# Products of zeros in TensorE's first waits, earlier column sums and a new place for one modulation tile per quarter, in a two-block transformer kernel

## The reference, cut to what matters

```python
c_act = jax.nn.silu(c)                                   # c: (1, 1024)
mod = jnp.einsum('bd,de->be', c_act, w_ada[l]) + b_ada[l]    # w_ada: (1024, 6 * 1024)
shift_m, scale_m, gate_m, shift_f, scale_f, gate_f = [m[:, None, :] for m in jnp.split(mod, N_MOD, axis=-1)]
h = (_rms(x) * (1.0 + scale_m) + shift_m).astype(dt)     # x: (1, 256, 1024)
proj = jnp.einsum('bsd,de->bse', h, w_in[l])             # w_in: (1024, 4104)
...
```

## Time and profile before

| | |
|---|---|
| median of 3 runs | 1022.15 us (1015.5 to 1022.82) |
| profiled execution, its own time | 1015.01 us |
| its span in the profile | 1013.2 us |
| TensorE busy (matmul) | 951.8 us, 94% |
| VectorE, ScalarE, GpSimd busy | 656.6, 485.2, 53.9 us |
| mean granted TensorE clock | 0.992 |
| read from HBM | 185.13 MB, 184 GB/s over the span |

### The profile page before, as it was taken

One profiled execution on the slowest core, in us unless ns is written; L12 is line 12 of the kernel. 1 busy time (PEld: TensorE's weight loads), 2 busy tenths in 40 slices (PEclk: granted clock), 3 DMA queues, 4 the chain that ended last, 5 costly groups with the idle time before them and its releaser, 6 DMA issues.

```text
span 1013.2 us, 14870 instructions
## 1 busy us (share of the span) xinstructions
PE 951.8 (94%) x5572; PEld 816.1 (81%) x5572; DVE 656.6 (65%) x828; ACT 485.2 (48%) x734; POOL 53.9 (5%) x59
## 2 busy tenths in 40 slices
PE   3889979799999999999899999998999989999996
PEld 3767867599999987977689999996776879999995
DVE  5778897886545575666884555558544876554555
ACT  5456646455444444444354544443653735444540
POOL 3030101100000001000020000001000010000000
PEclk9999989999999999999999999999999999999998
DMA  9998776776665576411476556544442447566531
GB/s 285 300 244 287 206 205 231 254 239 220 198 198 185 167 268 153 134 67 59 125 214 230 167 186 201 193 167 147 144 149 100 125 167 249 171 198 206 172 125 42
DMA packets 109991, 186.94 MB, mean 184 GB/s; under 512 B 8696, under 2 KB 67088, under 8 KB 109920
## 3 DMA queue, kind: packets, MB, share of 16 engines
q1 hardware_dynamic: 104800, 177.33, 54.2%
q0 software_dynamic: 2592, 8.53, 3.0%
q10 hardware_dynamic: 2544, 0.35, 0.2%
HBM read 185.13 MB, written 1.05 MB: 184 GB/s over the span
## 4 chain that ended last, share of the span: by engine, by line
PE 78%; DVE 9%; ACT 4%; issue 3%; DMA 2%; POOL 2%; SPq 0%; POOLq 0%; ACTq 0%; DVEq 0%
PE PJ L1766 14%; PE PJ L1767 13%; PE PJ L1768 13%; PE AT L1908 9%; PE AT L1907 9%; PE AT L1906 9%; DVE wlo L1107 2%; POOL rstd L467 2%; PE AT L1992 1%; DMA raw<-in_w_out_dram 1%; PE AT L2035 1%; PE AT L1757 1%; DMA raw<-in_w_in_dram 1%; DVE bn L1192 1%; DVE acc L1130 1%
## 5 line engine op out<-in xcount | busy, mean ns | idle before, releaser
L1107 DVE TENSOR_TENSOR wlo<-raw,whi 128x1024 fp32r<-128x1024 f32 x144 | 172.7, 1220 | 53.4 <-ACT whi L581 52.9
L1906 PE MATMUL AT<-hT_hi,whi 128*128 128x256 f32 x720 | 203.8, 283 | 0.0
L1908 PE MATMUL AT<-hT_hi,wlo 128*128 128x256 f32 x720 | 203.8, 283 | 0.0
L1907 PE MATMUL AT<-hT_lo,whi 128*128 128x256 f32 x720 | 203.7, 283 | 0.0
L1235 DVE TENSOR_TENSOR wlo<-raw,whi 128x1024 fp32r<-128x1024 f32 x144 | 169.8, 1221 | 33.1 <-ACT whi L639 32.6
L1766 PE MATMUL PJ<-whi,uhi 128*128 128x512 f32 x432 | 170.3, 394 | 1.7 <-DVE wlo L1107 0.9
L581 ACT ACTIVATE whi<-raw 128x1024 fp32r<-128x1024 f32 x144 | 146.7, 1054 | 49.4 <-DMA raw<-in_w_in_dram 29.3
L1767 PE MATMUL PJ<-wlo,uhi 128*128 128x512 f32 x432 | 168.7, 390 | 0.0
L1768 PE MATMUL PJ<-whi,ulo 128*128 128x512 f32 x432 | 168.2, 389 | 0.0
L639 ACT ACTIVATE whi<-raw 128x1024 fp32r<-128x1024 f32 x144 | 144.4, 1049 | 48.2 <-PE PJ L1768 44.3
L1766 PE MATMUL PJ<-whi,hT_hi 128*128 128x512 f32 (+1 forms) x320 | 132.3, 413 | 11.4 <-DVE hT_lo L1283 7.3
(11 more groups left out here) (310 smaller groups left out, 1054.8 us busy)
## 6 DMA issues: line engine op xcount, KB each, us to landing
raw<-in_mlp_w_dram SPq DMA_DIRECT2D x128, 512.0 KB, 4.9
raw<-in_w_in_dram SPq DMA_DIRECT2D x32, 512.0 KB, 6.0
raw<-in_w_ada_dram SPq DMA_DIRECT2D x32, 512.0 KB, 5.0
raw<-in_w_mlp_in_dram SPq DMA_DIRECT2D x32, 512.0 KB, 5.0
raw<-in_w_mlp_out_dram SPq DMA_DIRECT2D x32, 512.0 KB, 5.4
raw<-in_c_w_in_dram SPq DMA_DIRECT2D x24, 512.0 KB, 4.3
raw<-in_w_ada_dram SPq DMA_DIRECT2D x32, 256.0 KB, 6.0
raw<-in_a_w_in_dram SPq DMA_DIRECT2D x12, 512.0 KB, 5.0
```

What stands on the lines that cost most here:

```text
L1107: tt(wlo[:, n % SPL, :], raw_slot(r), whi[:, n % SPL, :].bitcast(F32), ALU.subtract).then_inc(raw_done, 1)
L1906: mm(o, whi[:, s % SPL, c], hT_hi[:, k, :], start=first, stop=False, skip_group_check=True)
L1907: mm(o, whi[:, s % SPL, c], hT_lo[:, k, :], start=False, stop=False, skip_group_check=True)
L1908: ins = mm(o, wlo[:, s % SPL, c], hT_hi[:, k, :], start=False, stop=last, skip_group_check=True)
```

## The change

There are four edits.

1. **Products of zeros.** VectorE zeroes the first 256 columns of `rows` and a half of `prT` as its first two instructions. TensorE waits for the first of them and multiplies 14 times a 128 x 128 part of `rows` by its 256 columns, float32, into bank 3 of `AT`, before its first wait for the constants. One such product stands between the second and the third group of transposes, 3 stand ahead of `mod_sums(0)` and 5 behind it. No result of them is read.
2. **The first odd half.** The first modulation tile's odd half is now added to the zeroed `prT` (`scalar_tensor_tensor`) where it was a plain multiplication (`tensor_scalar`).
3. **Column sums.** `mod_sums(g + 1)` stands ahead of the whole tile w(3g+2), no longer between its row tiles.
4. **One modulation tile per quarter.** In the list of fetches the order of a quarter is now w(3g), w(3g+1), one `ada`, w(3g+2), three `ada`. VectorE works for g = 1 and 2 up to and with that `ada` before it makes `h_low(g)`; that is one modulation tile that stood behind `h_low(g)`. ScalarE's order is the same as before.

```diff
--- before.py
+++ after.py
@@ -66,10 +66,12 @@
 
 def raw_plan():
 
-    seq = []
+    seq = [("ada", n) for n in range(4)]
     for g in range(BLK):
-        seq += [("ada", n) for n in range(4 * g, 4 * g + 4)]
-        seq += [("w", s) for s in range(FIRST_BLOCKS * g, FIRST_BLOCKS * (g + 1))]
+        s, n = FIRST_BLOCKS * g, 4 * (g + 1)
+        early = [("ada", n)] if g < BLK - 1 else []
+        late = [("ada", m) for m in range(n + 1, n + 4)] if g < BLK - 1 else []
+        seq += [("w", s), ("w", s + 1)] + early + [("w", s + 2)] + late
     n = ADA_FIRST
     for s in range(len(FIRST), T_END):
         seq.append(("w", s))
@@ -239,6 +241,7 @@
         acc_zero, ld_bada, ld_bada2 = sem("acc_zero"), sem("ld_bada"), sem("ld_bada2")
         xn_done, xt_tr, xt_done, modc_done = sem("xn_done"), sem("xt_tr"), sem("xt_done"), sem("modc_done")
         h0_hi, h0_32, h0_lo = sem("h0_hi"), sem("h0_32"), sem("h0_lo")
+        zeroed = sem("zeroed")
         ada_even = sem("ada_even")
         exp_c = sem("exp_c")
         cast_done = sem("cast_done")
@@ -1117,7 +1120,10 @@
                             stt(even, raw_slot(r)[:, 0:512], cvec[:, 3, 2 * q:2 * q + 1], even, ALU.mult, ALU.add)\
                                 .then_inc(ada_even, 1)
                             c = cvec[:, 3, 2 * q + 1:2 * q + 2]
-                            if q == 0:
+                            if q == 0 and g == 0:
+                                dve.wait_ge(zeroed, 2)
+                                stt(odd, raw_slot(r)[:, 512:], c, odd, ALU.mult, ALU.add).then_inc(raw_done, 1)
+                            elif q == 0:
                                 if g >= 2:
                                     dve.wait_ge(mod_mm, g - 1)
                                 ts(odd, raw_slot(r)[:, 512:], c, None, ALU.mult).then_inc(raw_done, 1)
@@ -1267,6 +1273,8 @@
                 square(MLP_STEPS - 1)
 
 
+            nc.vector.memset(rows[:, 0, 0:S], 0.0).then_inc(zeroed, 1)
+            nc.vector.memset(prT[:, 0, :], 0.0).then_inc(zeroed, 1)
             dve.wait_ge(exp_c, 1)
             link(ts(cvec[:, 1, :], cvec[:, 1, :], 1.0, None, ALU.add))
             link(nc.vector.reciprocal(cvec[:, 2, :], cvec[:, 1, :]))
@@ -1285,7 +1293,7 @@
 
             dve.wait_ge(ld_bada, 32)
             for g in range(BLK):
-                raw_to(W_AT[FIRST_BLOCKS * g + (g > 0)] + 1)
+                raw_to(W_AT[FIRST_BLOCKS * g + (g > 0)] + 1 + (0 < g < BLK - 1))
                 h_low(g)
                 raw_to(W_AT[FIRST_BLOCKS * g + 2] + 1)
             dve.wait_ge(ld_bada2, 16)
@@ -2167,21 +2175,31 @@
                 30: [scale_row],
             }
 
+            def zeros(n):
+
+                for _ in range(n):
+                    mm(AT[:, 3, 0:S], rows[:, 0, 0:P], rows[:, 0, 0:S], start=True, stop=True)
+
+            pe.wait_ge(zeroed, 1)
+            zeros(14)
             pe.wait_ge(ld_cst, 16)
             for q in range(4):
+                zeros(1) if q == 2 else None
                 pe.wait_ge(xn_done, q // 2 + 1)
                 for c in range(4):
                     ins = nc.tensor.transpose(PJ[:, q, c * P:(c + 1) * P], from_proj(q // 2, 4 * (q % 2) + c), ident)
                 ins.then_inc(xt_tr, 1)
+            zeros(3)
             mod_sums(0)
+            zeros(5)
             for s, (b, i) in enumerate(FIRST):
+                if b == FIRST_BLOCKS - 1 and i < BLK - 1:
+                    mod_sums(i + 1)
                 for t in range(NT):
                     if t == 0:
                         if b == 0:
                             pe.wait_ge(h0_lo, 2 * (i + 1))
                         pe.wait_ge(raw_done, raw_of(T_IN + s) + 1)
-                    elif b == FIRST_BLOCKS - 1 and i < BLK - 1:
-                        mod_sums(i + 1)
                     ins = tile_part(bank(b, t), T_IN + s, t, hT_hi, hT_lo, KPT * i, 512, i == 0, i == BLK - 1)
                 ins.then_inc(w_used, 1)
                 for step in between.get(s, ()):
```

## The result

| | before | changed |
|---|---|---|
| median of 16 runs | 1019.07 us | 1011.58 us |
| lowest and highest | 1014.24, 1022.82 | 1007.36, 1016.10 |
| ratio | | 0.9934, 95% interval 0.9917 to 0.9951 |
| profiled execution, its span | 1013.2 us | 1009.1 us |

The change makes the kernel 0.66% faster, 6.7 us by the ratio and 7.5 by the medians. The forecast was 4.2.

A forecast was written before the change was run, and what follows sets the result against it. TensorE, busy 94% of the span, was taken as the bound. Start 3.4, w0 2.4 and three quarters at up to 1.3, less a7's wait, came near 7.4; transfers left 4.2: 1022.15 - 4.2 = 1018.0 us, range 1008.5 to 1024.5.

The forecast's parts named there:

- The term for VectorE's first half: Start: a faster first odd half on VectorE lets the sums of quarter 0 start 1.6 us earlier, at 14.3.
- up to 1 us: Behind the sums of quarter 0: cost of the five products of zeros at the slow pace, without the expected cover.
- these 2.4 us: First weight tile w0: 12 matmuls at 0.23 us take 2.76 us instead of 5.2, so 2.4 us less.
- the mark: The start of w9, first tile of the last quarter, 60.12 us before; a gain there is carried to the end.
- The wait for a7: Ahead of the sums of quarter 1: TensorE waits 1.6 us for VectorE's modulation tiles, done at 27.1.
- The 10.6 us that I took for a quarter: Two further quarters: TensorE needs 10.2 us each, VectorE is busy 9.5; 10.6 taken with its short waits.
- The engines' bound: By the engines alone, w3 starts at 31.1 and w9 at 52.3, 7.8 us earlier.
- the transfers: Weight tile fetches up to w9: gain limited to between 2.3 and 7.4 us; 4.2 taken.
- TensorE and VectorE decide: Rival: the engines set the gain, -7.4 us, 1014.8; needs w4 and w7 landed some 5 us earlier; chance 0.15.
- Only the gaps close: Rival: the transfer stream keeps its pace and only its gaps close, -2.3 us, 1019.9; chance 0.2.
- The zeros don't raise the clock: Rival at the start: products of zeros stay slow, w0 starts 6 us late, +1.9 us, 1024; chance 0.1.
- The clock falls elsewhere: Rival: the clock's fall after the gap before 140.70 is shorter or longer, plus or minus 3.4 us; chance 0.1.

The follow-up runs named there:

- again: The changed kernel run once more, no edits; ratio to before 0.9937, w9 at 53.81 us.
- no5: The changed kernel without the five products of zeros behind the sums of quarter 0; ratio to before 0.9945.
- noZ: The changed kernel without its products of zeros, other edits kept; ratio to before 0.9936.
- noM: The changed kernel with the old order of fetches and the old place of h_low; ratio to before 0.9957.
- noC: The changed kernel with the column sums back between the row tiles of the third tile; ratio to before 0.9953.
- startonly: The kernel before with only the edits at the start: products of zeros and the adding first odd half; ratio to before 0.9982.
- noS: The changed kernel with the plain multiplication (tensor_scalar) for the first odd half; ratio to before 0.9959.
- quarters: The kernel before with only column sums ahead of the third tile and the moved modulation tile; ratio to before 0.9971.
- spread: The changed kernel with products of zeros redistributed: 12 at the start, one before each of the last three transpose groups, 5 ahead of quarter 0's sums, 3 behind; ratio 0.9945.
- dense: The changed kernel with the edits of spread, and the sums of quarter 1 alone back in the middle of w2; ratio to before 0.9936.
- both: The changed kernel with the edits of dense plus 8 products of constants in the idle 4.0 us near 129 us; ratio to before 0.9947.

## Why the prediction was right, and where its size was off

**The total.** 1018.0 us was forecast and 1011.58 measured, 6.4 less. 3.1 of them are the base: the median of before is 1022.15 over the three runs that I had and 1019.07 over 16. The other 3.3 are the gain, 7.5 us for 4.2. The range, 1008.5 to 1024.5, is so wide that it holds 1019.07, no change, as well; what bears the prediction out is the marks in the traces, below.

**The start.** Right. The term for VectorE's first half was 1.6 us; the sums started at 14.38 for 15.99. w0 at 19.1 was a forecast, 19.80 came. The difference is the case that I had priced as "up to 1 us": the clock fell at 16.7 and the five products ran slowly. In again it stayed at half for 6.8 us, and w0 started at 20.83. w0 took 3.05 us for the 5.2 of before, and 2.9 to 3.8 in six other runs with these products. But the sum counts these 2.4 us as a gain at the mark, and they are none: in no5 w0 ran at half pace and w9 came at 53.12. What the zeros bring at the mark is the faster sums of quarter 0, 1.96 us for the 3.59 of noZ, since the splits that free the slots of w3 and w4 stand behind them.

**The quarters.** Right in mechanism for quarters 2 and 3. The wait for a7 was there, 0.74 us for the 1.6 forecast. That 1.6 does not follow from its own terms, a7 done at 27.1 and w1 at 24.6: they give 2.5, or 1.8 if the sums wait for a7's even half alone, as they do in the trace. VectorE was done with a7 at 27.08, and TensorE with w1 at 25.73. The 10.6 us that I took for a quarter are 10.4 in the trace, and TensorE sets them, not VectorE: it is busy 20.63 of the 20.80 us, VectorE 17.91. The engines' bound was 31.1 for w3 and 52.3 for w9; 32.42 and 53.22 came. The moved tile cost the 0.2 us before w6 that I gave it (w5's last matmul at 42.36, w6 at 42.83), and 0.2 before w3 (3.04 us from the end of w4's rounding, 2.81 in noM). It brought 2.0, a gain for which the sum had no term of its own.

**The step that was mis-sized: the transfers.** The prediction let them leave 4.2 of 7.4 us, "nearer to the lower end, since the share of 1.00 says that the DMA engines had little room". The share said no such thing. In the changed kernel the queues moved 340 GB/s for 292 in the same two quarters at a share of 1.07. noC shows it from the other side: the same period as before with tiles 2 us earlier. And the row that I leaned on, w4's wait of 3.08 us at 32.41, stood for a slot that VectorE freed late: w4 came 4.0 us earlier once the start alone was earlier (startonly). What the transfers did take off the bound is w4 in quarter 1, 0.9 us at the mark and not 3.2. It is also why noZ, noS and quarters lost more than the engines' chains alone would have cost them. What the Trainium skill says in "SBUF — State Buffer", section "SBUF: two separate sides", that DMA and engines don't slow each other, is not contradicted by this: the slots changed, and the runs don't tell what the slower packets of before were due to.

**The rivals.** The one that came closest is "TensorE and VectorE decide", -7.4 us, to which I gave 0.15: w9 came 6.9 us earlier, and the medians differ by 7.5. "Only the gaps close" (2.3 us) is refuted by w4, w7 and w10, which came 4.1, 5.9 and 7.3 us earlier. "The zeros don't raise the clock" is refuted: it rose at 6.4 us, after 5.2 us of them. "The clock falls elsewhere" was meant of the fall behind the gap at 140.70, and that one stayed as it was, 6.8 us in both kernels. Behind 500 us it is true of single executions, and the likely reason why the profiled spans show 4.1 us of 6.9.

## What to carry to other kernels

A high DMA share with a low rate does not by itself show a limit. Ask which engine frees the slots, and test it by a run in which the tiles come earlier and the engines' chain is as it was; if the period stays, that chain sets it. Ask it for each stage: here the chain set quarters 2 and 3, and a transfer set quarter 1.

Column sums, transposes and other short work that a chain of three engines waits for belongs ahead of the block of matmuls that can cover the chain, and the data for it must be ready by then, or the whole block waits.

Products of zeros in a wait buy a faster next tile, but only if that tile is what the next step waits for; and the clock's fall moves, so look at several executions.

## What the runs showed of the hardware

- Products of zeros raise the granted clock: in the changed kernel it was at full speed from 6.4 us, after dense work since 1.20. Without them it rose at 24.9 in noZ. In quarters, which has none either, it rose at 13.7, behind the 16 transposes, fell at 17.1 and rose again at 27.4.
- In executions of the same code the clock fell at 16.7 us for 3.4 us (changed) and at 15.3 for 6.8 (again), each time during or right behind the column sums. With a denser stretch ahead it fell at 27.7 for 6.8 us (spread), at 29.4 for 6.8 (dense) and at 33.5 for 3.4 (both).
- A window shows a clock of 1.00 before its first event, at matmuls of half pace (before, up to 27.6 us). The pace is the surer sign.
- A VectorE memset beside a GpSimd memset took 0.27 us, while a plain multiplication beside one took 2.87 to 2.90 us in three kernels (before, noS, quarters), and 0.48 without it; the form that adds took 0.75 beside it. The Trainium skill, "SBUF — State Buffer", section "Who interferes with whom", has the multiplication among the operations that take the shared port pair; the trace agrees.
- The pace of transfers followed the slots: 292, 311 and 340 GB/s over the same two quarters in three kernels (before, noC, changed), at shares of 1.00, 1.02 and 1.07.
